# Relative-position bias by a stored band of 128 copies a head, read back straight into the table, in place of a one-row store and four flip matmuls

## The reference

```python
tbl = rel_bias.T.astype(jnp.float32)              # (8 heads, 32 buckets)
...
rel_own = t[:, None] - (blk * MOBA_BLOCK + r)[None, :]
s_own = (jnp.einsum('bhqd,bhrd->bhqr', qc, k_own).astype(jnp.float32) * scale
         + tbl[:, t5_bucket(rel_own)])
s_own = jnp.where(rel_own >= 0, s_own, NEG_INF)
```

## Time and profile before

| | before |
|---|---|
| median of 3 runs | 1063.08 us |
| the three runs | 1062.24, 1063.08, 1063.96 us |
| profiled execution, span | 1066.6 us (no other time is given for it) |
| PE busy | 1046.8 us, 98% of the span |
| DVE, ACT, POOL busy | 611.0, 447.1, 39.5 us |
| DMA | 191.46 MB, 180 GB/s over the span |

### The profile page before, as it was taken

How to read it: one execution, slowest core, us unless ns; L and a number is a source line. 1 busy time by engine, 2 the same in 40 slices (tenths; PEclk the granted TensorE clock), 3 DMA queues, 4 the chain that set the end, 5 groups by cost and what they waited for, 6 DMA issues and landing times.

```text
span 1066.6 us, 12641 instructions
## 1 busy us (share of the span) xinstructions
PE 1046.8 (98%) x4770; PEld 857.8 (80%) x4770; DVE 611.0 (57%) x705; ACT 447.1 (42%) x516; POOL 39.5 (4%) x53
## 2 busy tenths in 40 slices
PE   7999999999999899999999999999999899999998
PEld 5888888787878688888888888888888688888886
DVE  5645455864434755445586554545678765454574
ACT  5434344245433444434444444444254354344441
POOL 2100000100000100000010000000111100000010
PEclk9999999999957999999999999999999999999999
DMA  8855655446302576465546755545266575655531
GB/s 276 290 200 178 211 184 173 131 146 191 111 15 67 170 259 213 158 199 177 182 173 222 247 178 197 196 158 201 95 207 230 176 265 184 210 183 171 197 119 40
DMA packets 128914, 191.46 MB, mean 180 GB/s; under 512 B 5320, under 2 KB 95432, under 8 KB 128752
## 3 DMA queue, kind: packets, MB, share of 16 engines
q1 hardware_dynamic: 125952, 180.37, 50.5%
q0 software_dynamic: 2928, 10.61, 3.0%
HBM read 189.90 MB, written 1.06 MB: 179 GB/s over the span
## 4 chain that ended last, share of the span: by engine, by line
PE 91%; DVE 4%; DMA 2%; ACT 1%; issue 1%; SPq 0%; POOL 0%; DVEq 0%
PE gu L340 19%; PE gu L342 18%; PE gu L341 18%; PE acc L340 9%; PE acc L342 9%; PE acc L341 9%; PE tp L398 4%; DVE g_lo L913 2%; PE acc L542 2%; ACT g_hi L690 1%; DMA rawB<-in_ffn_w_up 1%; PE acc L539 1%; DMA rawB<-in_sgu_w_in 1%; DVE xT_lo L913 0%; DMA rawB<-in_sgu_w_out 0%
## 5 line engine op out<-in xcount | busy, mean ns | idle before, releaser
L340 PE MATMUL gu<-g_hi,xT_hi 128*128 128x512 f32 x928 | 364.4, 393 | 4.8 <-DVE xT_lo L913 3.3
L342 PE MATMUL gu<-g_hi,xT_lo 128*128 128x512 f32 x928 | 361.8, 390 | 0.0
L341 PE MATMUL gu<-g_lo,xT_hi 128*128 128x512 f32 x928 | 361.2, 389 | 0.0
L340 PEld LDWEIGHTS gu<-g_hi,xT_hi 128*128 128x128 f32 x928 | 174.2, 188 | 42.6 <-DVE xT_lo L913 4.2
L342 PEld LDWEIGHTS gu<-g_hi,xT_lo 128*128 128x128 f32 x928 | 174.2, 188 | 36.6
L341 PEld LDWEIGHTS gu<-g_lo,xT_hi 128*128 128x128 f32 x928 | 174.3, 188 | 35.5 <-issue 0.2
L739 ACT ACTIVATE stage<-gu 128x256 f32<-128x256 f32 x88 | 33.8, 384 | 377.6 <-PE gu L342 377.6
L913 DVE TENSOR_TENSOR g_lo<-rawA,g_hi 128x2048 fp32r<-128x2048 f32 (+1 forms) x63 | 142.1, 2256 | 82.6 <-ACT g_hi L690 82.6
L913 DVE TENSOR_TENSOR g_lo<-rawB,g_hi 128x2048 fp32r<-128x2048 f32 (+1 forms) x63 | 141.9, 2252 | 19.3 <-ACT g_hi L690 19.3
L1012 DVE SCALAR_TENSOR_TENSOR stage<-stage,gu 128x256 f32<-128x256 f32 x88 | 37.0, 421 | 194.4 <-ACT stage L739 194.4
L340 PE MATMUL acc<-d_hi,hT_hi 128*128 128x512 f32 x352 | 144.4, 410 | 0.0
(11 more groups left out here) (159 smaller groups left out, 711.5 us busy)
## 6 DMA issues: line engine op xcount, KB each, us to landing
rawD<-in_ffn_w_down SPq DMA_DIRECT2D x44, 1024.0 KB, 4.8
rawA<-in_ffn_w_gate SPq DMA_DIRECT2D x43, 512.0 KB, 3.7
rawA<-in_ffn_w_up SPq DMA_DIRECT2D x43, 512.0 KB, 4.7
rawB<-in_ffn_w_gate SPq DMA_DIRECT2D x43, 512.0 KB, 4.1
rawB<-in_ffn_w_up SPq DMA_DIRECT2D x43, 512.0 KB, 5.3
rawA<-in_attn_w_in SPq DMA_DIRECT2D x12, 512.0 KB, 4.3
rawB<-in_attn_w_in SPq DMA_DIRECT2D x12, 512.0 KB, 4.8
rawA<-in_ple_w_gate SPq DMA_DIRECT2D x8, 512.0 KB, 5.5
```

What stands on the lines that cost most here:

```text
L340: pe.matmul(dst, hi[b], w_hi[b], start=first and b == 0, stop=False)
L341: pe.matmul(dst, hi[b], w_lo[b], start=False, stop=False)
L342: done = pe.matmul(dst, lo[b], w_hi[b], start=False, stop=last and b == len(hi) - 1)
```

## The change

Each head's row (now 384 values: 256 by distance and 128 times -1e30) is stored 128 times, one behind the other, in `bias_rows` (8 by 128 by 384, 1.57 MB). A read that starts at element 127 and moves 383 elements a partition then lands one place earlier in the row for each next partition, so the band comes the right way up and goes straight into `bias_tab`. The `flip` matrix, the four flip matmuls, the four DVE copies and the semaphores around them go. POOL's store now waits for `d_done` at 8 as well, and the read follows right behind it; before, the read waited for `d_done` at 22. Head 0's addition on DVE waits for the read itself. One count of the constants that POOL makes goes down by one.

```diff
 ATTN_ORDER = [
-    ("g", 0, 0), ("half1",), ("flip",), ("g", 0, 1), ("turn", 0, 0), ("forget",),
+    ("g", 0, 0), ("half1",), ("g", 0, 1), ("turn", 0, 0), ("forget",),
...
-    bias_rows = nc.dram_tensor("bias_rows", (HEADS, 512), F32, kind="Internal").ap()
+    bias_rows = nc.dram_tensor("bias_rows", (HEADS, P, S + P), F32, kind="Internal").ap()
...
                         elif e[0] == "forget":
                             pe.wait_ge(f_split, 1)
-                            pe.wait_ge(bias_done, 1)
...
-                        elif e[0] == "flip":
-                            pe.wait_ge(bias_ld, 16)
-                            for q in range(4):
-                                done = pe.matmul(acc[q // 2][:, q % 2, :], flip[:, :],
-                                                 bias_rev[:, q // 2, 512 * (q % 2):512 * (q % 2) + 512],
-                                                 start=True, stop=True)
-                            done.then_inc(bias_flip, 1)
...
-                        elif e[0] == "flip":
-                            dve.wait_ge(bias_flip, 1)
-                            for q in range(4):
-                                done = dve.tensor_copy(bias_tab[:, 512 * q:512 * q + 512],
-                                                       acc[q // 2][:, q % 2, :])
-                            done.then_inc(bias_done, 1)
...
                                 if n == 0:
-                                    dve.wait_ge(bias_done, 1)
+                                    dve.wait_ge(bias_ld, 16)
...
             pool.wait_ge(bias_sb, 1)
-            pool.dma_start(bias_rows, bias_row_sb).then_inc(bias_st, 16)
+            pool.wait_ge(d_done, 8)
+            pool.dma_start(bias_rows, bias_row_sb[:, 0:S + P].unsqueeze(1).to_broadcast([HEADS, P, S + P]))\
+                .then_inc(bias_st, 16)
             pool.wait_ge(bias_st, 16)
+            pool.dma_start(bias_tab[:, :].rearrange("p (n u) -> p n u", u=S),
+                           bass.AP(bias_rows.tensor, P - 1, [[S + P - 1, P], [P * (S + P), HEADS], [1, S]]))\
+                .then_inc(bias_ld, 16)
...
-                    if ln == 0 and h == 0:
-
-                        pool.wait_ge(d_done, 2 * NCH)
-                        pool.dma_start(bias_rev[:, :, :].rearrange("p h (n u) -> p (h n) u", u=S),
-                                       bass.AP(bias_rows.tensor, 0, [[1, P], [512, HEADS], [1, S]]))\
-                            .then_inc(bias_ld, 16)
```

More of the change, by code:

```diff
@@ L156, in build @@
         ident = sb("ident", [P, P])
-        flip = sb("flip", [P, P])
         wf_raw = sb("wf_raw", [P, KB, HEADS])
@@ L182, in build @@
             head_c = sb("head_c", [HEADS, 2048], where=region)
-        bias_rev = v_att
         with ExitStack() as region:
@@ L230, in build @@
         const_ready, pool_step = sem("const_ready"), sem("pool_step")
-        bias_in, bias_mm, bias_sb, bias_st, bias_ld, bias_flip, bias_done = (
-            sem("bias_in"), sem("bias_mm"), sem("bias_sb"), sem("bias_st"), sem("bias_ld"), sem("bias_flip"),
-            sem("bias_done"))
+        bias_in, bias_mm, bias_sb, bias_st, bias_ld = (
+            sem("bias_in"), sem("bias_mm"), sem("bias_sb"), sem("bias_st"), sem("bias_ld"))
         f_loaded, f_hi, f_split, f_mm, f_exp, f_arg, f_ln, f_cum = (
@@ L535, in scores @@
                         if n == HEADS:
-                            pe.wait_ge(const_ready, 4)
+                            pe.wait_ge(const_ready, 3)
                         if g == 1:
@@ L1290, in _ @@
                                pattern=[[-1, P]], channel_multiplier=1).then_inc(const_ready, 1)
[L1291 to L1294, removed]
             pool.dma_start(rel_sb[:, :], rel_bias).then_inc(bias_in, 16)
@@ L1314, in _ @@
             pool.memset(sel_r[:, :].bitcast(F32), 0.0).then_inc(pool_step, 1)
-            pool.wait_ge(pool_step, 5)
+            pool.wait_ge(pool_step, 4)
             pool.affine_select(out=causal[:, :], in_=causal[:, :], compare_op=ALU.is_ge, fill=NEG, base=P,
```

## The result

| | before | after |
|---|---|---|
| median of 4 runs, alternating, us | 1063.45 | 1074.23 |
| lowest to highest, us | 1062.24 to 1063.96 | 1072.10 to 1076.26 |
| span of the profiled execution, us | 1066.6 | 1072.1 |
| busy time of PE in it, us | 1046.8 | 1040.9 |

The ratio is 1.0102, with a 95% interval of 1.0081 to 1.0124: the change makes the kernel 10.8 us slower. That is above the range of the prediction (1059.2 to 1068.0), on the side of its first rival, the held weight load, and beyond that rival's middle of 1069 us.

The account below looks back on a forecast made before the run. PE, busy 98% of the span, was taken as the bound. Removed flips gain 1.7 us, all else 0: 1063.08 - 1.7 = 1061.4 us (0.57), own range 1060.2 to 1062.6, range over all 1059.2 to 1068.0.

Parts of the forecast that it names:

- first rival, the held weight load: First ffn phase: the eight-partition store delays weight loads and PE waits; middle 8 us, giving 1069 us; chance 0.23.
- The attention start: Start of the attention phase: flips of 3.7 us go, about 2 us return as idle time, PE gains 1.7 us.
- POOL held nobody up: POOL's queue: store and read may take 98.9 us before the layer norm at 192.05 us; store's length alone costs nothing.
- cost of nothing for the four copies and for "forget": Attention start: removing DVE's four copies, 2.48 us, and the wait of "forget" for them was costed at nothing.
- What the store takes from the weights: First ffn phase: the store shares DMA engines with weight loads, which have free time and room to be late; cost 0.
- Read row by row the likeliest is nearer the lower end, 6 to 20 us: Store on POOL's queue: likeliest length 6 to 20 us, since nothing in the trace shows a transfer that crawls.
- The bound above, 75 us: Store on POOL's queue: upper bound on its length from reading 8 of 128 SBUF partitions, 21 GB/s.
- the rows at 554 us: Loads at 554 to 567 us: POOL loads 2 MB beside 2 MB of weights, ACT waited 0.3 us; nearest case.
- the prediction's estimate for two ports: Within the first rival: partitions 0 to 7 on two of sixteen ports, store 29 us, 18.6 us lost, 1080 us.
- price T - 10.4: First rival, first ffn phase: a store of length T makes a load take 5.3 + T, costing T - 10.4 us.
- PE's wait begins only when the load takes 15.7 us: First ffn phase: `rawB` load's lateness limit, from 11.56 us until ACT reads it and 4.14 us of ACT idle time.
- the precedent of the 1.62 us: Attention start: new idle time compared with 1.62 us at 367 us, behind which the clock stayed up.

Follow-up runs that it names:

- experiment 1: Kernel after, but with the old one-row store (8 rows of 2 KB) read straight into the table, band upside down: 1062.41 us, ratio 0.9977 to before.
- experiment 2: Kernel after, with the same 1.5 MB stored from all 128 partitions, 8 copies each: 1061.07 us, ratio 0.9973 to before.
- experiment 3: Kernel after, with the store's eight source partitions at 0, 4, ... 28 instead of 0 to 7: 1060.9 us, ratio 0.9972 to before.
- experiment 5: Kernel after, with the store's eight source partitions at 0, 16, ... 112: 1061.13 us, ratio 0.9979 to before.
- experiment 7: Kernel after, with each row stored once (12 KB) and the 128 copies made from device memory to device memory: 1060.07 us, ratio 0.9961 to before.
- experiment 4: Kernel before, flips kept, plus the large store from eight partitions at the same place into memory nobody reads: 1076.06 us, ratio 1.0105 to before.
- experiment 6: Kernel after, with the store from partitions 0 to 7 cut in two halves, at d_done 8 and 16: 1071.13 us, ratio 1.007 to before.

## Why the prediction was wrong, point by point

**The attention start was right.** PE was to be idle for 1.6 to 1.8 us behind the transposes, ended by `xT_lo`, and its second matmul to come 2.96 us after the first: it was 1.67 and 3.01. The gain of 1.7 us appears in the trace (1.70), and with the loads undisturbed or late without harm, in experiments 1, 2, 3, 5 and 7 as 1.9, 3.2, 3.4, 2.6 and 3.7 us of the medians, each with some 2 us of uncertainty. Their mean is 3.0. Where the 1.3 us above the place's own 1.7 come from stays open. It is hardly the clock in the heads: runs with the same mean granted clock, 0.984, differ by 2.8 to 3.7 us on average too. The wait of the flips for a late band, 0.4 us in experiment 4 and none in the profile before, can be a part. POOL held nobody up: store and read were over at 136 us, long before 192. The read took 8.4 us and not near 6. The cost of nothing for the four copies and for "forget" held as well, as far as PE shows no gap there.

**The step that failed is "What the store takes from the weights", with its "So I take 0 here".** Two readings stand behind it. The first: "Read row by row the likeliest is nearer the lower end, 6 to 20 us" for the store. It took 34.1 us. The bound above, 75 us, was worked out from the share of partitions, and the reason given against it, that nothing in the trace crawls, was no reason: no transfer of the trace reads a few partitions many times. The second: the rows at 554 us were taken as precedent. There 2 MB go into all 128 partitions, and experiment 2 shows 1.5 MB out of all 128 at no cost; the rows say what many bytes do beside the weights, and nothing on a slow source.

How the length comes about is shown by four points, the same 1,572,864 bytes from source partitions that lie differently:

| source partitions | ports, by the map of the Trainium skill | store, us | GB/s a port, 1.8 us for the start taken off |
|---|---|---|---|
| 0 to 7 | 2 | 34.1 | 24 |
| 0, 16, ... 112 | 4 | 21.2 | 20 |
| 0, 4, ... 28 | 8 | 12.2 | 19 |
| all | 16 | 7.2 | 18 |

(The 1.8 us is what the 16 KB store took in experiment 1; 1.57 MB / 32.3 us / 2 = 24 GB/s.) Each doubling takes off 13, 9 and 5 us, and 8 partitions take 34.1, 21.2 or 12.2 us by where they lie. That 0, 16, ... 112 are slower than 0, 4, ... 28, though they lie further apart and in eight different groups of four as well, speaks for the map of ports and not for mere distance. Why the rate of a port falls down the table was not tried; the weights, which want the same engines, may be it. "SBUF — State Buffer" of the Trainium skill, in the section named above, is what this bears out: by its figure the prediction's estimate for two ports was 29 us, 5 below the measured 34.1. The other rule that the prediction cited, in "DMA: Bandwidth & Descriptors" of the Trainium skill, that an outermost dimension below 16 confines a DMA to as many engines, does not set the time alone: it is the same for the three kernels with eight source partitions, and their times differ by up to a factor of 2.8. But the traces don't speak against it. In the midst of the store its packets took 48.0% of the sixteen engines' time in the kernel after (96 to 125 us), 44.0% with four ports and 43.6% with eight, which is 7.7, 7.0 and 7.0 engines' worth; with all 128 partitions as outermost dimension it was 84.2%, or 13.5. By this estimate the source was narrow in two ways: the ports set how long the store takes, and it kept about eight engines busy, no more.

That the held load is the mechanism is shown by experiment 4 (the store alone makes the gap) with experiments 2, 3 and 7 (a quicker store, no gap). Inside it one thing is only inferred: `rawA`, issued 1.8 us behind the store, lands 1.5 us behind it (34.1 and 33.8 us from their issues). That fits loads whose pieces on those engines stand behind the store's; no view shows a single engine, and why the load issued at 94.42 got through in 7.7 us was not followed.

**The rival had the right mechanism and a wrong price rule.** The prediction named the held load, the loads issued at 95 us as the first to look at, and PE's gap in the first ffn phase. Its price T - 10.4 rested on "PE's wait begins only when the load takes 15.7 us": the load was said to be due when ACT's next gate is. But ACT's gate is only late work at that point; PE needs its outcome half a chunk later, after the product that it is in. Beside the gate at 106.87 of the earlier trace rows, the timelines of PE and ACT before show:

```profile
115.09 0.38 PE L398 MATMUL tp<-ident,stage 128*128 128x128 f32 x2
...
115.28 0.39 ACT L739 ACTIVATE stage<-gu 128x256 f32<-128x256 f32 x1 [5.87 <-PE gu L342]
```

PE takes the gate of 106.87 at 115.09, 8.2 us later. (The 15.7 us are also those of `rawB`; for `rawA`, which was held, the same rule gives 12.0 + 5.9 = 17.9 us: issued at 95.48, read at 107.50, with 5.87 us of idle time behind.) Read backwards from 123.06, where PE runs dry, `stage` (0.41), the low part (2.29) and the high part (1.91) must fit, so the load must have landed by 118.45, 23.5 us after its issue at 94.89. 33.8 - 23.5 = 10.3 us, where 10.34 were measured; that agreement is by construction, since both are read from one trace. The test is experiment 5, from one side: its 21.2 us are below the 23.5 and cost nothing. With the measured 34.1 the old rule gives 23.7 us, twice the loss. Of the 13.4 us that this is above the 10.3 us of idle time, 7.8 come from the tolerance of 15.7 in place of 23.5, and 5.6 from adding the usual 5.3 to the store's length, where the load took 33.8 and not 39.4. The length was guessed at half and its price at double, and that the rival's middle of 8 us comes near the measured 10.8 is luck.

**Not priced at all: the clock behind the gap.** "The new idle time ahead of the product has the precedent of the 1.62 us" was true for that gap, behind which the clock stayed up again. Behind 10.34 us of idle time it was 1.2 GHz for 4.2 us of work, which costs half of that, 2.1 us. 10.3 + 2.1 = 12.4 of the 12.8 us that the place cost; the rest was not followed. The head loop had the low clock for less time than before, 34.1 us against 41.0, and not for more.

**The chances.** 0.23 for the held load was too little for what the prediction itself had in hand: a ceiling of 75 us from rows, an estimate of 29 us, and a deadline of 15.7. By its own numbers every store above 10.4 us cost something, and of the 6 to 20 us that it guessed two thirds lie above that; the range should have reached past 1080.

## What to carry to other kernels

A store that repeats a few rows is costed by where its rows lie in SBUF and not by its bytes alone: here 1.5 MB took 7, 12, 21 or 34 us from all partitions, from every fourth up to 28, from every sixteenth, and from the first eight; and the quick ways were to lay the rows on more partitions first, or to store them once and make the copies in device memory. A slow transfer is not hidden because nobody waits for it: list the loads that run beside it, and let each be as late as the transfer is long. For the price of a late load follow it to the engine that bounds the kernel, through all that stands in order behind it, and count from the moment at which that engine runs dry, not from the first engine that waits.

## What was not expected of the hardware

- While the slow store ran, SP's queue took 3.95, 10.52 and 8.41 us for single issues that take 0.37 to 0.46 otherwise. The load issued at 115.62 was therefore late from the start, though the timeline shows SP waiting for no semaphore. Experiments 4 (3.94, 11.05, 8.57) and 5 (3.60, 2.36, 4.67) show the same.
- After 10.3, 10.5 and 6.0 us of idle time of PE (the kernel after, experiments 4 and 6) the granted clock was 1.2 GHz for 4.2, 3.3 and 6.0 us of work; after 1.6 to 1.7 us it stayed at 2.4 GHz. But in the profile before it was 1.2 GHz from 353.0 to 356.4 us, behind waits of only 1.18 and 0.79 us, and behind the same two waits in the profile after it stayed up.
- The low clock in the heads lasted 41.0 us in the profile before, and 23.9 to 37.5 in the nine others. At half the clock that is up to 8.6 us of time: a difference of two profiled spans below some 9 us is therefore no verdict on an edit here.
- The band read, 5.9 us at its old place, took 6.2 to 9.1 us right behind a store issued at 93 us, beside the weights, and cost PE nothing there; in experiment 6, behind the second half, it took 9.6.
